# Queries and keys of two prompt tiles by seven half products, prompt latents through memory, last expert block in column halves

## The reference

```
u = h @ w_in                 # (1024+32, 1024) x (1024, 2208)
q_sb, k_sb, v_sb, q_lat, kv_lat, kpe_raw = split(u)   # 512,512,512,384,256,32
q_sb, k_sb = rmsnorm per head of 64
qm = rmsnorm(q_lat) @ w_qb;  kv = rmsnorm(kv_lat) @ w_kvb
```

## Time and profile before

| what | us |
|---|---|
| three runs, median (lowest to highest) | 1279.31 (1279.07 to 1280.71) |
| the profiled execution's own time | 1286.58 |
| its span | 1285.0 |
| PE busy in it | 1179.3 (92%) |
| DVE, ACT, POOL busy | 675.9, 356.2, 211.7 |
| mean granted clock of PE | 0.961 |

### The profile page before, as it was taken

How to read it: one execution, slowest core, us unless ns; L and a number is a source line. 1 busy time by engine, 2 the same in 40 slices (tenths; PEclk the granted TensorE clock), 3 DMA queues, 4 the chain that set the end, 5 groups by cost and what they waited for, 6 DMA issues and landing times. The chain is left out here.

```text
span 1285.0 us, 19035 instructions
## 1 busy us (share of the span) xinstructions
PE 1179.3 (92%) x7176; PEld 661.3 (51%) x7177; DVE 675.9 (53%) x1329; ACT 356.2 (28%) x782; POOL 211.7 (16%) x249
## 2 busy tenths in 40 slices
PE   4999999999987997899999999899976998999995
PEld 1455555555543565666677767555543332343331
DVE  1255444554465784567777776544472343553533
ACT  1122222222222444156555544223331000000000
POOL 4000000000000002254434333010122121212111
PEclk9899999999997998889999999899987999999998
DMA  8721211111136882421111005362576999999983
GB/s 361 300 65 35 66 48 51 54 45 54 33 117 210 309 290 66 106 77 30 30 30 30 2 1 164 100 252 84 181 268 200 390 379 351 370 389 384 360 302 62
DMA packets 92835, 213.48 MB, mean 166 GB/s; under 512 B 20673, under 2 KB 54707, under 8 KB 77394
## 3 DMA queue, kind: packets, MB, share of 16 engines
q1 hardware_dynamic: 82274, 195.02, 41.6%
q0 software_dynamic: 7200, 17.33, 5.5%
q10 hardware_dynamic: 3280, 0.02, 0.1%
HBM read 185.03 MB, written 34.13 MB: 171 GB/s over the span
## 5 line engine op out<-in xcount | busy, mean ns | idle before, releaser
L1944 PE MATMUL f_C<-first_region,oT 128*128 128x512 f32 x256 | 115.1, 602 | 0.0
L455 PE MATMUL U<-region,b_hT 128*128 128x512 f32 x256 | 112.3, 592 | 0.0
L2702 DVE TENSOR_TENSOR g_sig<-g_GU,g_sig 128x256 f32<-128x256 f32 x23 | 9.8, 424 | 158.1 <-ACT g_sig L2653 158.1
L2488 PE MATMUL g_GU<-late,first_region 128*32 128x512 f32 (+2 forms) x384 | 88.0, 609 | 4.3 <-issue 4.3
L2488 PE MATMUL g_GU<-w_gu,first_region 128*32 128x512 f32 (+2 forms) x448 | 86.1, 604 | 6.3 <-issue 5.2
L1724 DVE TENSOR_TENSOR_SCAN region<-region,early 128x128 f32<-128x128 f32 (+7 forms) x64 | 88.6, 1404 | 6.2 <-POOL region L1531 6.2
L455 PE MATMUL b_UL<-region,b_hT 128*128 128x384 f32 (+1 forms) x256 | 76.7, 460 | 3.3 <-DMA region<-w_in 3.3
L1944 PEld LDWEIGHTS f_C<-first_region,oT 128*128 128x128 f32 x256 | 48.0, 193 | 54.2 <-issue 54.1
L455 PEld LDWEIGHTS U<-region,b_hT 128*128 128x128 f32 x256 | 47.6, 190 | 54.1 <-issue 54.0
L2467 POOL DMA_INDIRECT y<-oT,g_li x23 | 36.4, 1584 | 226.0 <-DVE oT L2720 200.4
L1593 PE MATMUL e_Z<-first_region,region 104*128 104x512 f32 (+3 forms) x192 | 70.5, 505 | 0.3 <-ACT region L1686 0.3
(11 more groups left out here) (515 smaller groups left out, 2215.6 us busy)
## 6 DMA issues: line engine op xcount, KB each, us to landing
region<-w_ada SPq DMA_DIRECT2D x16, 1024.0 KB, 6.3
late<-w_gate SPq DMA_DIRECT2D x14, 1024.0 KB
late<-w_up SPq DMA_DIRECT2D x14, 1024.0 KB
late<-w_down SPq DMA_DIRECT2D x14, 1024.0 KB
w_gu<-w_gate SPq DMA_DIRECT2D x12, 1024.0 KB
w_gu<-w_up SPq DMA_DIRECT2D x12, 1024.0 KB
w_down<-w_down SPq DMA_DIRECT2D x12, 1024.0 KB, 22.4
region<-w_in SPq DMA_DIRECT2D x3, 2048.0 KB, 17.4
```

The costliest lines, as they stand in the source:

```text
L455: end = nc.tensor.matmul(dst[0:T, 0:c1 - c0], lhsT=hT[:, k, 0:T], rhs=g.w_in[:, k, c0:c1], start=k == 0, stop=k == KD - 1)
L1944: end = nc.tensor.matmul(C[n % 2][:, c * 512:(c + 1) * 512], lhsT=g.oT[:, i, k, :], rhs=wo[:, k, c * 512:(c + 1) * 512], start=k == 0, sto ...
L2488: end = nc.tensor.matmul(GU[h * n:h * n + n, :], lhsT=xT[:, b, k, h * n:h * n + n], rhs=wgu[s][:, :, k, :], start=k == 0, stop=k == KD - 1 ...
L2702: mark(nc.vector.tensor_tensor(sig[:], GU[:, 0:DE], sig[:], ALU.mult))
```

## The change

Queries and keys of two prompt tiles become one 2x2 problem: two tiles of rows, two halves of the contraction (512 each), two column groups (queries, keys). Eight half products (four contraction steps each) become seven, on sums of the inputs and of the weights. DVE forms four input sums per pair and combines the products out of PSUM by seven additions; ACT copies one of them out. The four weight sums, each 512x512, are made once in the first tile, two by DVE and two by POOL, in `first_region`. The w_in parts come as latents, values, queries, keys; the input of the second tile is loaded ahead of queries and keys. In even tiles `hT_of(i+1)` goes before the values, in odd ones behind the transposes of the latents. All tiles are written out.

The prompt's values, latent values and latent keys no longer stay in SBUF: they are stored per tile and read back (2 MB, 2 MB and 3 MB) behind the load of `ckv_s`, and POOL and PE wait for them at the start of `phase_e`. The mask rows are written at the end of `phase_b`'s products. At the end of `phase_b` SP also waits for the new stores. The last expert block is weighted and added into y in two halves of 512 columns, each with its own index list.

The diff, cut to its core:

```diff
-W_IN_PARTS = ((3 * SBW, INC), (0, SBW), (SBW, 2 * SBW), (2 * SBW, 3 * SBW))
+W_IN_PARTS = ((3 * SBW, INC), (2 * SBW, 3 * SBW), (0, SBW), (SBW, 2 * SBW))
+PROD = 7
...
-            step(nc.gpsimd.memset(g.hidden[:], 0.0))
...
+        HALF = KD // 2
+        kept = [g.first_region[:, h * TOK:h * TOK + SEQ] for h in range(MH)]
+        sums = [kept[2 * j:2 * j + 2] for j in range(4)]
+        w_sum = [[sums[j][k // 2][:, k % 2 * 512:k % 2 * 512 + 512] for k in range(HALF)] for j in range(4)]
+        sticks = g.values[:, 0:PT * SBW]
+        latents = g.values[:, NT * SBW:NT * SBW + PT * SBW]
+        hTs = [m.sb("b_hT", [P, KD, P])[:], sticks[:, 0:D].rearrange("p (k t) -> p k t", t=P)]
+        qks = [m.sb("b_qk", [P, 2 * SBH, SBD])[:], sticks[:, D:2 * D].rearrange("p (h d) -> p h d", d=SBD)]
+        h_sum = sticks[:, 2 * D:4 * D].rearrange("p (j k t) -> p j k t", j=4, t=P)
+        kmT = latents[0:MK, 0:D].rearrange("p (h t) -> p h t", t=P)
+        v_out, vm_out, part, first_sum = (latents[:, D + j * 512:D + j * 512 + 512] for j in range(4))
+        second_sum, third_sum = g.early[:, 0:512], g.early[:, 512:1024]
+        hT, qk = hTs[0], qks[0]
...
+        U2_AT, C11_AT, V5_AT, U3_AT, C22_AT, C12_AT, C21_AT = range(1, PROD + 1)
+        def tiles(body):
+            for i in range(PT):
...
+            def latents_out(i):
+                sp.wait_ge(e4, i + 1)
+                sp.wait_ge(e5, i + 1)
+                sp.dma_start(g.km_dram[:, :, i * P:(i + 1) * P], kmT).then_inc(st_km, 16)
...
+            def body(i):
                 sp.wait_ge(kpe_done, i + 1)
                 sp.dma_start(out("o_ckv", i), ckv[:]).then_inc(st_ckv, 16)
                 sp.dma_start(out("o_kpe", i), kpe[:, ROPE:2 * ROPE]).then_inc(st_kpe, 16)
...
+                if not second(i):
+                    rows_in(i + 2)
+                sp.wait_ge(v_evac, i + 1)
+                sp.dma_start(out("o_v", i), v_out).then_inc(st_v, 16)
+                if i:
                     queries_out(i - 1)
...
+                    latents_out(i - 1)
+                if second(i) and i + 2 <= PT:
+                    rows_in(i + 2)
+                keys_out(i)
+                sp.wait_ge(kv_evac, i + 1)
+                sp.dma_start(g.vm_dram[i * P:(i + 1) * P, :], vm_out).then_inc(st_vm, 16)
...
+            rows_in(1)
...
+        @block.gpsimd
+        def _(pool):
...
+            pool.wait_ge(in_k, 16)
+            for k in range(0, HALF, 2):
+                end = nc.gpsimd.tensor_tensor(sums[2][k // 2].rearrange("p (s n) -> p s n", s=2),
+                                              g.w_in[:, HALF + k:HALF + k + 2, SBW:2 * SBW],
+                                              g.w_in[:, k:k + 2, SBW:2 * SBW], ALU.subtract)
+            end.then_inc(t_late, 1)
+            pool.wait_ge(in_q, 16)
+            pool.wait_ge(t_early, 2)
+            for k in range(0, HALF, 2):
+                end = nc.gpsimd.tensor_tensor(sums[3][k // 2].rearrange("p (s n) -> p s n", s=2),
+                                              g.w_in[:, HALF + k:HALF + k + 2, 0:SBW],
+                                              sums[1][k // 2].rearrange("p (s n) -> p s n", s=2), ALU.subtract)
+            end.then_inc(t_late, 1)
+            pool.wait_ge(prod_mm, PROD * PT // 2)
+            step(nc.gpsimd.memset(g.hidden[:], 0.0))
...
+            def product(dst, rows, weights):
+                for k in range(HALF):
+                    end = nc.tensor.matmul(dst[:, :], lhsT=rows[:, k, :], rhs=weights(k), start=k == 0,
+                                            stop=k == HALF - 1)
+                end.then_inc(prod_mm, 1)
...
+            def body(i):
...
+                project(i, UL[:, 0, :], 3 * SBW, 3 * SBW + QR, None, first)
+                project(i, UL[:, 1, :], 3 * SBW + QR, INC, lat_mm)
+                if not first:
+                    back(i - 1, 0)
+                if not second(i):
+                    if first:
+                        pe.wait_ge(ht_first, KD)
+                    hT_of(i + 1)
+                    pe.wait_ge(c_out, PROD * ((i + 1) // 2))
+                project(i, U2, 2 * SBW, 3 * SBW, v_mm)
+                if not first:
+                    back(i - 1, 1)
+                if not second(i):
+                    a, b = hTs
+                    A11, A12, A22 = a[:, 0:HALF], a[:, HALF:], b[:, HALF:]
+                    q, k_ = slice(0, SBW), slice(SBW, 2 * SBW)
+                    S1, S2, S3, S4 = (h_sum[:, j] for j in range(4))
+                    pe.wait_ge(ht_done, i + 1)
+                    if first:
+                        pe.wait_ge(in_q, 16)
+                    product(U[0], A11, lambda k: g.w_in[:, k, q])
+                    if first:
+                        pe.wait_ge(t_early, 2)
+                    pe.wait_ge(h_sums, 4 * p + 3)
+                    product(U[1], S2, lambda k: w_sum[1][k])
+                    pe.wait_ge(part_out, p + 1)
+                    product(U[0], A12, lambda k: g.w_in[:, HALF + k, q])
+                    pe.wait_ge(v_evac, i + 1)
+                    product(U2, S1, lambda k: w_sum[0][k])
+                    latents_turned(i)
+                    if first:
+                        pe.wait_ge(t_late, 1)
+                        pe.wait_ge(in_k, 16)
+                    pe.wait_ge(c_out, PROD * p + U2_AT)
+                    product(U[1], S3, lambda k: w_sum[2][k])
+                    pe.wait_ge(h_sums, 4 * p + 4)
+                    pe.wait_ge(c_out, PROD * p + V5_AT)
+                    product(U2, S4, lambda k: g.w_in[:, HALF + k, k_])
+                    if first:
+                        pe.wait_ge(t_late, 2)
+                    pe.wait_ge(c_out, PROD * p + C22_AT)
+                    product(U[1], A22, lambda k: w_sum[3][k])
+                else:
+                    latents_turned(i)
+                    pe.wait_ge(c_out, PROD * (p + 1))
+                    hT_of(i + 1)
...
+                if i:
+                    back(i - 1, (0,))
+                if second(i):
+                    x_stats(i + 1)
+                    qk_norms(i)
+                    qk_roots(i)
+                values_out(i)
+                if i:
+                    back(i - 1, (1,))
+                if not second(i):
+                    act.wait_ge(prod_mm, PROD * p + 1)
+                    nc.scalar.activation(part, U[0][:, :], ACT.Copy).then_inc(part_out, 1)
+                latents_out(i)
+                if not second(i):
+                    qk_norms(i)
+                    qk_roots(i)
...
+            def weights_summed():
...
+                dve.wait_ge(in_k, 16)
+                for k in range(0, HALF, 2):
+                    end = nc.vector.tensor_tensor(sums[0][k // 2].rearrange("p (s n) -> p s n", s=2),
+                                                  g.w_in[:, k:k + 2, SBW:2 * SBW], g.w_in[:, k:k + 2, 0:SBW],
+                                                  ALU.subtract)
+                end.then_inc(t_early, 1)
+                dve.wait_ge(t_early, 1)
+                for k in range(0, HALF, 2):
+                    end = nc.vector.tensor_tensor(sums[1][k // 2].rearrange("p (s n) -> p s n", s=2),
+                                                  g.w_in[:, HALF + k:HALF + k + 2, SBW:2 * SBW],
+                                                  sums[0][k // 2].rearrange("p (s n) -> p s n", s=2), ALU.subtract)
+                end.then_inc(t_early, 1)
+            def rows_summed(i):
+                p = i // 2
+                a, b = hTs
+                dve.wait_ge(ht_done, i + 1)
+                nc.vector.tensor_tensor(h_sum[:, 0], b[:, 0:HALF], b[:, HALF:], ALU.add).then_inc(h_sums, 1)
+                nc.vector.tensor_tensor(h_sum[:, 2], a[:, 0:HALF], b[:, 0:HALF], ALU.subtract).then_inc(h_sums, 1)
+                dve.wait_ge(h_sums, 4 * p + 1)
+                nc.vector.tensor_tensor(h_sum[:, 1], h_sum[:, 0], a[:, 0:HALF], ALU.subtract).then_inc(h_sums, 1)
+                dve.wait_ge(h_sums, 4 * p + 3)
+                nc.vector.tensor_tensor(h_sum[:, 3], a[:, HALF:], h_sum[:, 1], ALU.subtract).then_inc(h_sums, 1)
+            heads = lambda ap: ap.rearrange("p (h d) -> p h d", d=SBD)
+            def combine(i, at):
+                p = i // 2
+                if at == U2_AT:
+                    dve.wait_ge(part_out, p + 1)
+                    dve.wait_ge(prod_mm, PROD * p + 2)
+                    end = nc.vector.tensor_tensor(first_sum, part, U[1][:, :], ALU.add)
+                elif at == C11_AT:
+                    dve.wait_ge(st_k, 16 * i)
+                    dve.wait_ge(prod_mm, PROD * p + 3)
+                    end = nc.vector.tensor_tensor(qks[0][:, 0:SBH, :], heads(part), heads(U[0][:, :]), ALU.add)
+                elif at == V5_AT:
+                    dve.wait_ge(prod_mm, PROD * p + 4)
+                    dve.wait_ge(c_out, PROD * p + U2_AT)
+                    end = nc.vector.tensor_tensor(second_sum, first_sum, U2[:, :], ALU.add)
...
```

(55 more changed lines are left out.)

277 lines of the change are left out of this document (144 added, 133 removed).

## The result

The changed kernel takes 1286.17 us in the median of 8 runs (1283.16 to 1289.1), the kernel before 1279.78 beside it: ratio 1.0047, 95% interval 1.003 to 1.0064, so 6.0 us slower where 4.7 us faster was forecast, and outside the range.

A forecast was written before the change was run, and what follows sets the result against it. PE alone was taken to bound the projection stage. Terms -13.7 + 4.6 + 3.1 + 2.0 + 0.5 - 1.25 = -4.75 us gave a median of 1274.6 us, 0.37% faster; range 1270.0 to 1281.8.

The forecast's parts named there:

- Half products: Prompt projections of queries and keys: seven half products instead of eight in each of four pairs save 3.43 each, -13.7 us.
- the odd tiles: Latent transposes in odd tiles wait about 0.5 us for a bank that ACT empties, four times, +2.0 us.
- POOL's mask work: Mask fill moved to POOL behind the last product, covered by later tiles: 0; uncovered some 13 us.
- The first tile's wait and the clock: First tile: PE waits for the second tile's scaled input, +4.6 us, then runs at low clock, +3.1 us.
- Sums of weights and inputs: First tile's weight sums on DVE and POOL and DVE's input sums stay hidden behind PE's work: 0 us.
- Rival (2): DVE and POOL stop each other in the sums, delaying the second product: up to 4, taken as 2.5 us; chance 0.12.
- Stores: Extra stores per tile delay the projection stage's end, in front of the sample's last stores: +0.5 us, bounds 0 to 1.5.
- Writing out the tiles: Projection stage: writing out all prompt tiles instead of looping repeats existing code and costs 0 us.
- Last block: Last expert block: weighting and scattering in two column halves shortens the end, -1.25 us.
- Read-back: Reading back 7.3 MB behind ckv_s ends near 509, before its first reader at 541.17: 0; uncovered 17.8 us.
- rival (4): Sample attention: read-back overtakes the cached latents, PE waits 5.9 us plus some 2 at low clock, 1282.5 us; chance 0.12.

The follow-up runs named there:

- a_shift: Changed kernel plus 48 tiny useless transposes (96 instructions) in PE's projection stage, where PE waits for DVE anyway; ratio to the kernel before 0.9987.
- a_shift128: Changed kernel plus 128 tiny useless transposes (256 instructions) at the same place as in a_shift; ratio to the kernel before 1.0054.
- bu_readback: b_unrolled plus the change's extra stores and the 7.3 MB read-back with its waits, full products kept; ratio to the kernel before 1.0003.
- a_best: a_start with the last store of latent keys issued behind the sample's stores and waited for only ahead of the read-back; 1268.85 us, ratio to before 0.9912.
- b_shift: Kernel before plus the same 48 tiny transposes at the same place as in a_shift; ratio to the kernel before 0.9982.
- b_unrolled: Kernel before with only the eight prompt tiles of the projection stage written out instead of looped; ratio to the kernel before 0.9977.
- a_start: a_both with POOL's first weight sum also behind DVE's input sums, plus the 48 transposes of a_shift; 1270.0 us, ratio to before 0.9919.
- a_both: Changed kernel with POOL's second weight sum after the first input sums and the second tile's input scaled before the first latents' norms; ratio to before 1.0015.

## Why the prediction was wrong

**Half products, as forecast.** The second and third pair are 82.0 - 79.1 = 2.9 us shorter each, by 3.43 less the price of the odd tiles (a wait of 0.34 in each). The last is 2.2 shorter; it holds a wait of 0.39 more, beside POOL's mask work, which the forecast had at 0. The first is 6.9 longer (89.4 against 82.5), which is 3.8 shorter without the 10.8 us of waiting and low clock below; 1.2 of these are luck, the first latent projection at 11.0 instead of 12.2. In all 11.8 where -13.7 and +2.0 make 11.7.

**The first tile's wait and the clock, right in size.** 4.47 against 4.6. The slower transposes and values cost 0.9 + 2.15 = 3.05 against 3.1.

**Sums of weights and inputs, "0": wrong.** The step took DVE's instructions at the price that they have alone and set POOL beside them as free. Rival (2) had the mechanism, its place and 2.5 us; the wait measured 3.25 and 2.53 in the two profiles of the changed kernel (4.29 and 4.02 in a_shift and a_shift128). It had 0.12, too little for something that the one row with both engines, spoke for and that only needed to be scheduled against.

**Stores, "+0.5": 1.5.** The upper bound given there: bu_readback, with the stores alone, has it, and a_best, with the last one out of the way, is rid of it. SP's issues stand in line at the stage's end and had no slack.

**"Writing out the tiles repeats what tiles 0 and 7 already are: 0": this step failed most.** It priced the instructions that PE executes, not where all later ones then lie. *Small* went from 14.2 to 18.1, +3.9; the same code 96 instructions further takes 11.7. a_shift, a_shift128, b_shift and bu_readback separate it from the read-back, the extra work and the loop. Writing out the tiles is only one part of what moves the code; alone, in b_unrolled, it moved it to a good place. No case held it.

**Last block, -1.25:** measured -1.1 at full and -2.2 at low clock.

**Read-back, 0:** right, and rival (4) is out: the latents landed after 8.3. The last part came 8 us later than worked out, the queues moving 213 to 284 GB/s from 500 to 515 and not the 411 of rows 6; it had the slack.

**The range.** The bounds named for the clock, the odd tiles, the stores and the end add up, as they are worded, to some 1268.4 to 1279.5, not 1269.8 to 1280.6. The measured time lies outside both.

**The account.** From the means of two profiles each: tiles -0.8, stage end +1.5, small +3.9, end -1.1 to -2.2; in all 2.4 to 3.5 of the 6.0 measured, whose interval starts at 3.8. Against the forecast -4.75 the steps that failed are some 3.2 in the tiles (the lock), 1.0 in the stores and 3.9 in *small*. *Rest* doesn't differ between the kinds (before and its variants 724.6 to 728.9, after and its variants 724.0 to 728.0). The shift experiments bear *small* out in size: it differs by 6.4 between after and a_shift, whose times differ by 7.4, and by 2.5 between before and b_shift, whose times differ by 2.3; but with *tiles* the rows make 4.8 and 3.8, so rows and times agree to some 2 us and no better. The 2.5 to 3.6 us that are left of the 6.0 stay open. a_start and a_best show what the idea is worth once the start and the code's place are in order: a_best is 9.0 us under b_shift (ratios 0.9912 and 0.9982). The forecast of 4.75 held 7.7 us of waiting and low clock at the start that a_best is mostly rid of, so it isn't borne out by this, only its direction.

## What to carry to other kernels

When DVE and POOL both get new sums of operands in SBUF, price each at the time beside the other (here 2.84 for 0.69), and order them so that the one that PE waits for runs alone. When an edit changes how many instructions an engine has, everything behind it moves against the boundaries at which its code arrives: look for idle put down to "issue" within a line that can wait for nothing, and try the same kernel with some harmless instructions ahead before judging the edit. "Issue" alone proves nothing: in the expert stage, whose products have weights to wait for, every kernel here has idle of 1 to 5 us under that name, before and after. Compare profiles stretch by stretch, never by their totals, where runs scatter by more than the effect.

## What was not expected of the hardware

- A stall of 4.2 to 4.8 us of PE at one fixed matmul in five profiles, gone with 96 instructions more ahead of it and back with 256. It comes while the attention stage's loads still fill the DMA queues, in the block where PE's instructions are shortest (128 matmuls of 64 columns in 1.99 us, each with its weight load). With its aftermath at half clock it is worth 6.4 us, more than the whole change was to bring.
- A milder form, with the queues empty by then: a gap of 0.57 to 0.99 us, and behind it 128 such matmuls at half clock, 3.58 instead of 1.99 us.
- DVE waits for whole instructions of POOL: 2.84 instead of 0.69 for 512 columns, 6.70 instead of 2.36 for two of 1024, when POOL started first.
- Removing a wait brought the lock forward (a_both): 4.5 us of idle went, 6.7 came.
